# Two transformer blocks on one core: norms with tokens on partitions in the delta rule and in forgetting attention, another rule for placing the first stage's small steps, and the pooled products one chunk sooner

## What is computed

```python
fq = rmsnorm(heads(fq, FOX_HEADS), fox_qnorm[l])
fk = rmsnorm(heads(fk, FOX_HEADS), fox_knorm[l])
...
ya = fox_attention(fq, fk, heads(fv, FOX_HEADS), logf)
...
def step(state, xs):
    q_n, u_n, w_n, g_n, attn_n, kt_n, gl_n = xs
    v_new = u_n - jnp.einsum("bhck,bhkv->bhcv", w_n, state)
    o = (jnp.einsum("bhck,bhkv->bhcv", q_n * jnp.exp(g_n)[..., None], state)
         + jnp.einsum("bhce,bhev->bhcv", attn_n, v_new))
    state = state * jnp.exp(gl_n)[..., None, None] + jnp.einsum("bhck,bhcv->bhkv", kt_n, v_new)
    return state, o
...
yb = (rmsnorm(o, gdn_onorm[l]) * jax.nn.silu(heads(gz, GDN_HEADS).astype(f32)))
...
mixed = (g[..., 0, :] * (ya @ w_oa[l]) + g[..., 1, :] * (yb @ w_ob[l])
         + g[..., 2, :] * (yc @ w_oc[l]))
```

## Time and profile before

| | |
|---|---|
| median of 3 runs | 1172.26 us (1172.22 to 1172.81) |
| the profiled execution, whole | 1173.59 us |
| its span, first to last instruction | 1171.9 us |
| mean granted TensorE clock | 0.995 |
| PE busy | 1149.0 us, 98% |
| DVE busy | 811.6 us, 69% |
| ACT busy | 620.9 us, 53% |
| POOL busy | 81.9 us, 7% |

### The profile page before, as it was taken

One profiled execution on the slowest core, in us unless ns is written; L12 is line 12 of the kernel. 1 busy time (PEld: TensorE's weight loads), 2 busy tenths in 40 slices (PEclk: granted clock), 3 DMA queues, 4 the chain that ended last, 5 costly groups with the idle time before them and its releaser, 6 DMA issues.

```text
span 1171.9 us, 16827 instructions
## 1 busy us (share of the span) xinstructions
PE 1149.0 (98%) x6777; PEld 1003.8 (86%) x6777; DVE 811.6 (69%) x880; ACT 620.9 (53%) x799; POOL 81.9 (7%) x114
## 2 busy tenths in 40 slices
PE   8999999999999999999999999999999999999997
PEld 7978998889987899999888888888777888888886
DVE  6897668756877668787458777547776747777743
ACT  7666446436477566565345444436456547444432
POOL 7101100200000000000000000002600000000000
PEclk9999999999999999999999999999999998999999
DMA  8654233334664445654656655655633534666560
GB/s 259 193 156 149 96 108 109 108 109 155 221 198 146 144 162 164 196 184 177 220 175 188 207 180 181 214 180 188 197 108 127 180 108 127 192 202 182 178 214 36
DMA packets 144420, 193.95 MB, mean 166 GB/s; under 512 B 6168, under 2 KB 121240, under 8 KB 144344
## 3 DMA queue, kind: packets, MB, share of 16 engines
q1 hardware_dynamic: 143144, 188.43, 49.9%
q0 software_dynamic: 1200, 4.46, 1.1%
HBM read 191.82 MB, written 1.05 MB: 165 GB/s over the span
## 4 chain that ended last, share of the span: by engine, by line
PE 83%; DVE 9%; ACT 4%; issue 3%; DMA 0%; DVEq 0%; ACTq 0%
PE banks L1344 23%; PE banks L1378 19%; PE banks L1326 13%; PE banks L1347 11%; PE banks L1363 3%; DVE wlo L1956 3%; PE banks L1354 2%; PE banks L1615 1%; ACT whi L1675 1%; PE banks L1502 1%; PE banks L1489 1%; PE banks L1392 1%; PE banks L1573 1%; PE banks L1333 1%; PE banks L1570 0%
## 5 line engine op out<-in xcount | busy, mean ns | idle before, releaser
L1956 DVE TENSOR_TENSOR wlo<-raw,whi 128x2048 fp32r<-128x2048 f32 (+1 forms) x178 | 406.6, 2292 | 123.9 <-ACT whi L1675 123.8
L1675 ACT ACTIVATE whi<-raw 128x2048 fp32r<-128x2048 f32 (+1 forms) x179 | 340.1, 1903 | 252.8 <-PE banks L1347 147.3
L1344 PE MATMUL banks<-xhl,whi 128*128 128x512 f32 x1232 | 396.5, 403 | 1.6 <-DVE y5l L2289 1.3
L1347 PEld LDWEIGHTS banks<-xhl,wlo 128*128 128x128 f32 x1232 | 231.4, 188 | 54.6
L1347 PE MATMUL banks<-xhl,wlo 128*128 128x256 f32 x1232 | 242.6, 278 | 0.0
L1344 PEld LDWEIGHTS banks<-xhl,whi 128*128 128x128 f32 x1232 | 189.0, 189 | 8.7 <-issue 5.8
L1326 PE MATMUL banks<-xhl,whi 128*128 128x256 f32 x912 | 165.5, 284 | 1.1 <-DVE xhl L1984 0.6
L1326 PEld LDWEIGHTS banks<-xhl,whi 128*128 128x128 f32 x912 | 142.0, 192 | 2.0 <-DVE xhl L1984 1.0
L1326 PE MATMUL banks<-xhl,wlo 128*128 128x256 f32 x456 | 129.0, 283 | 0.0
L1378 PE MATMUL banks<-whi,hh 128*128 128x512 f32 x264 | 102.9, 390 | 0.0
L1378 PE MATMUL banks<-wlo,hh 128*128 128x512 f32 x264 | 102.7, 389 | 0.0
(11 more groups left out here) (369 smaller groups left out, 1537.1 us busy)
## 6 DMA issues: line engine op xcount, KB each, us to landing
raw<-in_w_in SPq DMA_DIRECT2D x40, 1024.0 KB, 5.3
raw<-in_w_up SPq DMA_DIRECT2D x22, 1024.0 KB, 5.4
raw<-in_ffn_w_gate SPq DMA_DIRECT2D x22, 1024.0 KB, 5.3
raw<-in_ffn_w_up SPq DMA_DIRECT2D x22, 1024.0 KB, 5.3
raw<-in_ffn_w_down SPq DMA_DIRECT2D x22, 1024.0 KB, 5.1
raw<-in_w_down SPq DMA_DIRECT2D x11, 1024.0 KB, 5.1
raw<-in_w_out SPq DMA_DIRECT2D x8, 1024.0 KB, 5.2
raw<-in_xa_wkv SPq DMA_DIRECT2D x8, 1024.0 KB, 5.5
```

The source lines that it names most:

```text
L1344: pe.matmul(bank(b[m]), wh[:, k, m * P:(m + 1) * P], both[:, k, :, :].rearrange("p a t -> p (a t)"), start=(k == 0), stop=(k == KD - 1), s ...
L1347: ins = pe.matmul(bank(b[m])[:, 0:T], wl[:, k, m * P:(m + 1) * P], Xh[:, k, :], start=False, stop=(k == KD - 1), skip_group_check=True)
L1675: act.activation(columns(whi, c, part), columns(raw, c, part), ACT.Copy).then_inc(act_done, 1)
L1956: dve.tensor_tensor(columns(wlo, c, part), columns(raw, c, part), columns(whi, c, part), ALU.subtract).then_inc(dve_done, 1)
```

## The change

- **Forgetting attention's norms.** The fq and fk projections become V chunks, tokens on partitions, and so are copied out by ACT and not added by DVE. `token_norm` squares them on ACT, sums each head on DVE (`tn_red`), takes the root of 8 numbers a token on ACT, multiplies on DVE (`tn_mul`), and PE turns the eight 128x128 blocks (`tn_t`), which ACT writes out with the gain (`tn_e`). The four `hn` norms with their matmuls by ones go.
- **The delta rule's end.** gz becomes a V chunk pair. `g_bc`, `g_egc` and `g_qg`, which spread exp(g) over the partitions and scaled q, go: exp(g) comes as a fourth column of `gcols` and the last decay by one small matmul in `rows6`; `r_ws` also makes q times the state, with tokens on partitions, `r_q` scales it on ACT, and `r_oc` adds it on DVE. The norm of the result is `n_sq`, `n_red`, `n_r`, `n_mul`, with 128 tokens on partitions; for the first tile it rides on links of `gdn(1)`. At the end `n_t` turns both tiles, and `n_h` and `n_l` write the two parts directly; `hn("go0", "go1")` and the `yh`, `yl` of this branch go.
- **The placing of links** in the first stage: `EARLY["rows"]` and `EARLY_LONG` become 0, the rough costs are edited, and `drain()` before the O chunks goes: the long chain has to be finished only for the third branch.
- **`mem_load`** is issued after the third branch's first O chunk and not after the first branch.
- **The mixer.** `pl_mm` moves from the middle of the third qk chunk to the middle of the second V chunk, into banks 2 and 3, and the hook between `pl_h` and `pl_l` goes. In both MoBA lanes `pn` of the first head joins the link of its `sc`.
- `g_vb` and `z_lk` do the same work with fewer DVE instructions.

The diff, cut to its core (the table of rough costs and declarations of tiles are left out):

```diff
-EARLY, EARLY_LONG = {"rows": 0.5, "mem": 0.5, "moba": 0.5, "xa": 0.5}, 0.6
+EARLY, EARLY_LONG = {"rows": 0.0, "mem": 0.5, "moba": 0.5, "xa": 0.5}, 0.0
...
     for what, c0 in (("fq", FQ), ("fk", FK)):
-        for i in range(2):
-            wide(win, c0 + 256 * i, "x", "add", to=what, i=i)
+        vals(win, c0, "x", "vcopy", to=what)
...
-    for i in range(2):
-        wide(win, GZ + 256 * i, "x", "add", to="gz", i=i)
+    vals(win, GZ, "x", "vcopy", to="gz")
...
-                            i=i, banks=(2 * i, 2 * i + 1), evac="gated"))
+                            i=i, banks=(2 - 2 * i, 3 - 2 * i), evac="gated"))
...
-    ready = {f"y{br}": [("yl", br)] for br in range(3)}
+    ready = {f"y{br}": [("yl", br)] for br in (0, 2)}
+    ready["y1"] = [("n_l", 0), ("n_l", 1)]
...
+        if name == "tn_t":
+            return pl.ended.get(("hn_mul", "gk1"), 1e9)
...
+        if name == "n_mul":
+            return pl.ended.get(("gzs",), 1e9)
...
+    def token_norm(m):
+
+        return [[("act", "tn_sq", m), ("dve", "tn_red", m), ("act", "tn_r", m)], [("dve", "tn_mul", m)],
+                [("pe", "tn_t", m), ("act", "tn_e", m)]]
+
...
-        c += [[("pe", "g_uw", t), ("dve", "g_u", t), ("act", "g_w", t)],
-              [("pe", "g_bc", t), ("act", "g_egc", t), ("dve", "g_qg", t)]]
-        c += [[("pe", "r_ws", t), ("dve", "r_vn", t)],
-              [("pe", "r_o", t), ("act", "r_oc", t), ("dve", "r_s", t)]]
+        c += [[("pe", "g_uw", t), ("dve", "g_u", t), ("act", "g_w", t)]]
+        c += [[("pe", "r_ws", t), ("dve", "r_vn", t), ("act", "r_q", t)],
+              [("pe", "r_o", t), ("dve", "r_oc", t), ("dve", "r_s", t)]]
         return c
+
+    def delta_out(t):
+
+        return [("act", "n_sq", t)], [("dve", "n_red", t)], [("act", "n_r", t)], [("dve", "n_mul", t)]
 
...
+        if kind == "moba":
+            links = [links[0] + links[1]]
...
     a += hn("gq0", "gk0", "gq1", "gk1")
-    for t in range(2):
-        a += gdn(t)
-    a += hn("go0", "go1")
+    a += gdn(0)
+    second = gdn(1)
+    for link_, norm_ in zip(second, delta_out(0)):
+        link_ += norm_
+    a += second
+    n_sq, n_red, n_r, n_mul = delta_out(1)
+    a += [n_sq + n_red + n_r, n_mul, [("pe", "n_t", 0), ("pe", "n_t", 1), ("act", "n_h", 0), ("dve", "n_l", 0), ("act", "n_h", 1), ("dve", "n_l", 1)]]
...
-    b += hn("fq0", "fq1", "fk0", "fk1")
+    b += token_norm("fq") + token_norm("fk")
...
-    drain()
+    for t in range(2):
+        pl.take(("n_t", t), (4 + t,), ("n_l", t))
...
-        if nth == 0:
-            pl.add("act", "yh", BRANCHES[2])
-            pl.add("dve", "yl", BRANCHES[2])
...
-        if nth == 0:
-            pl.add("pool", "mem_load")
         if nth == 1:
             pl.add("dve", "premix")
+        if nth == 2:
+            pl.add("pool", "mem_load")
         c += 2
...
     mm(c)
-    mm(c + 1)
-    pl.take(("pl_mm",), (0, 1), ("pl_l",))
-    mm(c + 2, mid=[("pe", "pl_mm"), lambda: low_part(True), ("act", "pl_h"), hook, ("dve", "pl_l")])
+    pl.take(("pl_mm",), (2, 3), ("pl_l",))
+    mm(c + 1, mid=[("pe", "pl_mm"), lambda: low_part(True), ("act", "pl_h"), ("dve", "pl_l")])
+    mm(c + 2)
     mm(c + 3)
...
-            return bank(g % 2)[:, (g // 2) * T:(g // 2 + 1) * T]
+            return bank(2 + g % 2)[:, (g // 2) * T:(g // 2 + 1) * T]
...
-                pool.wait_ge(pe_done, at("mm", chunk_of("gated", 1) - 4, 1))
+                pool.wait_ge(pe_done, at("mm", chunk_of("gated", 1) - 1, 1))
...
-                    for j, row in enumerate((BETA, BEGC, ETAIL)):
-                        o = (t * 3 + j) * 4
-                        ins = pe.transpose(bank(4)[:, o:o + 4], row[:, t * P:(t + 1) * P], ident[0:4, 0:4])
-                ins.then_inc(pe_done, 1)
+                    for j, row in enumerate((BETA, BEGC, ETAIL, EGC)):
+                        o = (t * 4 + j) * 4
+                        pe.transpose(bank(4)[:, o:o + 4], row[:, t * P:(t + 1) * P], ident[0:4, 0:4])
+                pe.matmul(bank(4)[:, 32:40], ones[0:4, :], last_decay, start=True, stop=True).then_inc(pe_done, 1)
...
+            def tn_t(m):
+
+                pe.wait_ge(dve_done, at("tn_mul", m))
+                if m == "fq":
+                    pe.wait_ge(dve_done, at("hn_mul", "gk1"))
+                else:
+                    pe.wait_ge(act_done, at("tn_e", "fq"))
+                src = TO[m]
+                for t in range(NT):
+                    for h in range(NH):
+                        ins = pe.transpose(bank(6 + t)[:, h * P:(h + 1) * P], src[:, t, h * P:(h + 1) * P], ident[:, :])
+                ins.then_inc(pe_done, 1)
...
             def r_ws(t):
                 pe.wait_ge(act_done, at("g_w", t))
-                pe.wait_ge(dve_done, at("g_qg", t))
+                pe.wait_ge(dve_done, at("g_u", t))
+                s = slice(t * P, (t + 1) * P)
                 for h in range(NH):
-                    ins = pe.matmul(bank(4)[:, h * P:(h + 1) * P], gU[:, h, :], gS[:, h, :], start=True, stop=True)
+                    pe.matmul(bank(4)[:, h * P:(h + 1) * P], gU[:, h, :], gS[:, h, :], start=True, stop=True)
+                for h in range(NH):
+                    ins = pe.matmul(bank(5)[:, h * P:(h + 1) * P], gq_[:, h, s], gS[:, h, :], start=True, stop=True)
                 ins.then_inc(pe_done, 1)
 
             def r_o(t):
-                s = slice(t * P, (t + 1) * P)
                 pe.wait_ge(dve_done, at("r_vn", t))
+                pe.wait_ge(act_done, at("r_q", t))
                 for h in range(NH):
-                    o = bank(5)[:, h * P:(h + 1) * P]
-                    pe.matmul(o, gS[:, h, :], gq_[:, h, s], start=True, stop=False)
-                    pe.matmul(o, gMs0[:, h, :], gAT[:, h, :], start=False, stop=True)
+                    pe.matmul(bank(5)[:, h * P:(h + 1) * P], gAT[:, h, :], gMs0[:, h, :], start=True, stop=True)
                 for h in range(NH):
                     ins = pe.matmul(bank(4)[:, h * P:(h + 1) * P], gKt[:, h, :], gMs0[:, h, :], start=True, stop=True)
+                ins.then_inc(pe_done, 1)
+
+            def n_t(t):
+
+                pe.wait_ge(dve_done, at("n_mul", t))
+                pe.wait_ge(dve_done, at("r_s", 1))
+                for h in range(NH):
+                    ins = pe.transpose(bank(4 + t)[:, h * P:(h + 1) * P], go_[:, t, h * P:(h + 1) * P], ident[:, :])
                 ins.then_inc(pe_done, 1)
...
-                    pe.wait_ge(dve_done, at("hn_mul", "fk1"))
-                    pe.wait_ge(dve_done, at("hn_mul", "gk1"))
+                    pe.wait_ge(act_done, at("tn_e", "fk"))
...
+            def tn_sq(m):
+
+                act.wait_ge(act_done, at("copy", chunk_of(m, None)))
+                if m == "fk":
+                    act.wait_ge(dve_done, at("tn_red", "fq"))
+                act.activation(S1[:, :], TO[m][:, 0, :], ACT.Square)
+                act.activation(PT1[:, :], TO[m][:, 1, :], ACT.Square).then_inc(act_done, 1)
+
+            def tn_r(m):
+                act.wait_ge(dve_done, at("tn_red", m))
+                link(act.activation(token_root, token_root, ACT.Ln, bias=eps, scale=1.0 / HD))
+                act.activation(token_root, token_root, ACT.Exp, scale=-0.5).then_inc(act_done, 1)
+
+            def tn_e(m):
+
+                act.wait_ge(pe_done, at("tn_t", m))
+                act.wait_ge(dve_done, at("params_c"))
+                gain = gsc if m == "fq" else pcolumn("fox_knorm")
+                for t in range(NT):
+                    ins = act.activation((fq_ if m == "fq" else fk_)[:, :, t * P:(t + 1) * P], per_head(bank(6 + t)), ACT.Copy, scale=gain)
+                ins.then_inc(act_done, 1)
...
+                if t and l == 1:
+                    act.wait_ge(dve_done, at("n_red", 0))
...
+            def r_q(t):
+                act.wait_ge(pe_done, at("r_ws", t))
+                for h in range(NH):
+                    hs = slice(h * P, (h + 1) * P)
+                    ins = act.activation(go_[:, t, hs], bank(5)[:, hs], ACT.Copy, scale=gcols[:, t, 3, h:h + 1])
+                ins.then_inc(act_done, 1)
+
+            def n_sq(t):
+
+                act.wait_ge(dve_done, at("r_oc", t))
+                act.activation(gU[:, :, :], per_head(go_[:, t, :]), ACT.Square).then_inc(act_done, 1)
+
+            def n_r(t):
+                act.wait_ge(dve_done, at("n_red", t))
+                link(act.activation(onr[t], onr[t], ACT.Ln, bias=eps, scale=1.0 / HD))
+                act.activation(onr[t], onr[t], ACT.Exp, scale=-0.5).then_inc(act_done, 1)
+
+            def n_h(t):
+                act.wait_ge(pe_done, at("n_t", t))
+                act.wait_ge(pe_done, at("z_o", NH - 1))
+                act.activation(ybh[1][:, :, t * P:(t + 1) * P], per_head(bank(4 + t)), ACT.Copy,
+                               scale=pcolumn("gdn_onorm")).then_inc(act_done, 1)
...
+                for t in range(NT):
```

(50 more changed lines are left out.)

78 lines of the change are left out of this document (29 added, 49 removed).

## The result

The changed kernel takes 1182.89 us (median of 4, 1180.70 to 1183.35) against 1172.53 us: a ratio of 1.0082, 95% interval 1.0068 to 1.0095. That is 10.4 us slower, where I had forecast 10 us faster. The profiled execution took 1182.82 us, its span 1181.1 us.

The account below looks back on a forecast made before the run. PE was taken as the bound, busy 1149.0 of 1171.9 us. Terms -5.5 (PE work), -1.2 (placing) and -3.3 (mixer) sum to -10.0 us; from the median 1172.26 that gives 1162.3 us, range 1159.2 to 1168.0.

Parts of the forecast that it names:

- PE work, -5.5: Mostly first-stage PE instructions that go and come, such as hn_sum, g_bc and transposes: -5.5 us, hardly depending on the order.
- The -1.2 us that the placing was to win from waits: First stage: links placed only when their input is there win part of 1.8 us of PE waits: -1.2 us.
- So I let every `l_x` of both tiles slip once, and five others: Delta rule's long chain: 17 missed quarters at 1.4 us, 24 us later, less savings, ending near 282 us.
- five others: Five links of the long chain besides the l_x, each slipping once at 1.4 us.
- That is why the missing `drain()` costs nothing: After the gates: the chain ends 18 us before the third branch needs it, so dropping drain() costs nothing.
- The rival "slower": Chain not done when the third branch is due, links forced with PE idle; with eight, 1182 us. Chance 0.03.
- The tables among the sigmoids: Rival: n_r of the second tile after the first gsig, two more ACT table loads, 2 x 1.28 us: 1164.9 us. Chance 0.14.
- The mixer, -3.3: Second block's mixer: potential of 4.6 us from two waits and slow clock, 1.3 given back: -3.3 us.
- The 1.34 us may thus shrink or stay: Mixer: PE's 1.34 us wait for pl_l before the last qk chunk was to shrink or stay.
- The 1.7 us of slow clock: Mixer: 1.7 us lost to PE's clock of 0.66 after the wait before pt; was to go with that wait.
- `mem_load`: Issued three O chunks later, at 307 us, with 16 us to land before ACT reads the memory: cost 0.

Follow-up runs that it names:

- a_old_mixer: The changed kernel with the second block's mixer as before the change: 1179.77 us, ratio 1.0058.
- d_three_costs: The changed kernel with old placing and old mixer, and only the costs cv_add, cv_silu and hn_mul at their old values: 1167.12 us, ratio 0.9951.
- c_old_costs: The changed kernel with old placing, old mixer and all fifteen edited costs of steps that both kernels have at their old values: 1171.12 us, ratio 0.9988.
- d_old_costs_placing_03: c_old_costs with EARLY for the rows at 0.3 in place of 0.5: 1165.81 us, ratio 0.9941.
- a_old_both: The changed kernel with both the old placing and the old mixer, new costs kept: 1173.59 us, ratio 1.0006.
- d_drain: The changed kernel with drain() put back after the gates and nothing else: 1187.51 us, ratio 1.0128.
- a_old_placing: The changed kernel with EARLY for the rows back at 0.5 and EARLY_LONG at 0.6, drain() still missing: 1176.33 us, ratio 1.0031.
- c_best_merge: c_old_costs with one part of the new mixer, pn in the link of its sc: 1172.43 us, ratio 0.9998.
- e_after_old_costs: The changed kernel with the fifteen old costs and nothing else, new placing and new mixer kept: 1181.01 us, ratio 1.0060.
- e_03_mixer: d_old_costs_placing_03 with pn in its sc's link and no hook between pl_h and pl_l, pl_mm at its old place: 1165.31 us, ratio 0.9929.
- e_03_nohook: d_old_costs_placing_03 with only the hook between pl_h and pl_l taken out, no merge of pn: 1166.24 us, ratio 0.9939.
- d_three_costs_mixer: d_three_costs with pn in its sc's link and no hook between pl_h and pl_l, pl_mm at its old place: 1165.34 us, ratio 0.9939.

## Why the prediction was wrong

Step by step from the changed kernel: the mixer costs 3.1 us (a_old_mixer), placing and three costs together 1179.8 - 1167.1 = 12.7 us (from there to d_three_costs), and what is left is 1167.1 - 1172.85 = -5.7 us, the last against the kernel before on the same chip. I had -3.3, -1.2 and -5.5. (The top of my range should have read 1168.3 by its own sum; the measured time is far above either.)

- **PE work, -5.5: right in kind, a little small.** d_three_costs is 5.3 us ahead at norm_mem's turn and 5.7 in the median, but its first stage has 3.4 us of waits against 2.0 before. From 55 us to that turn PE is busy for 263.6 us against 270.4, both at a clock of 1.00, so its work is 6.8 us less, and the nearness of 5.7 to my 5.5 is in part luck. Nor is it true that this part hardly depends on the order: the same instructions take 264.6 us in c_old_costs and 262.2 in d_old_costs_placing_03. The -1.2 us that the placing was to win from waits didn't come. The token norms don't make the chain late.
- **"So I let every `l_x` of both tiles slip once, and five others": this step failed.** I took 24 us of slip, less 5 and 4, and an end near 282 us. `g_uw` of the second tile alone came 39.3 us late. The levels did what I had said: the second tile's six `l_x` take 36.6 us (243.3 to 279.9) against 29.4 (211.2 to 240.6), 1.4 us a step, and both tiles' together 14.3 us more, where I had 12 x 1.4 = 16.8. The "five others", 7 us in my sum, are what was mis-sized: the first tile's `g_turn` is 15.2 us late already, and from its `g_uw` to the second tile's first `l_x` it takes 62.7 us (180.6 to 243.3) against 50.4 (160.8 to 211.2), 12.3 us more. With the three costs undone `g_turn` stands at 101.4 us instead of 117.4 (d_three_costs and a_old_both), so the first piece lies in the steps ahead of it, the convolution (`cv_add`, `cv_silu`) and the norms of q and k (`hn_mul`). Of the 9 us that I took off the chain (5 for `g_bc`, 4 for the result's norm) little came at its end: from the second tile's `g_uw` to the end of the norm it takes 20.7 us (282.1 to 302.8) against 23.8 (242.9 to 266.6). Why a link loses more than the quarter that it misses stays my reading, that it has several DVE or ACT steps; no run has it alone. I treated the placing as one number that each link meets once. It acts through the planner's clocks together with the cost table, and that table, part of the change, has no term in my sum at all. Undone singly in the changed kernel, the costs are worth 1.9 us, which the intervals don't tell from nothing, and the placing 6.6; undone together (three costs) 12.7.
- **"That is why the missing `drain()` costs nothing": right for the wrong reason.** The chain was not done 18 us before the 300.5 us at which I had the branch start, but at 305.6, 5 us after, and PE had no weight product left from 291.2 us on; the missing drain then saved 4.6 us (d_drain).
- **The rival "slower", 0.03, is what happened,** at 1182.9 us to my 1182. Its price was partly luck: I had eight forced links at 2.5 us, and there were three, with 11.0 us of idle PE, a clock near half from 295 to 310 us, and two table loads and `premix` inside. Its condition, a chain 34 us later, was the right one, and I gave it too little since my slip had no row under it.
- **The tables among the sigmoids** came too, as part of that wait: 2 x 1.28 us before `n_mul`. The load at 306.57 us is the one that the kernel before has at 302.88.
- **The mixer, -3.3: wrong sign, 2.7 to 3.1 us lost.** The wait before `pt` shrank from 1.51 to 0.75 us; I had it gone. The failed step is the place of `pl_l`: "The 1.34 us may thus shrink or stay". It grew to 2.84 us. In a_old_placing, whose wait is the same (2.82), `pl_mm` is done at 847.2, but ACT has the next chunk's `hi` and two lane steps (a copy of PT and an `ex`) ahead of `pl_h`, which starts only at 849.26, and `pl_l` ends at 852.60 (in the changed kernel the same: 852.7, 854.80 and 858.13):

```profile
845.78 1.90 ACT L1708 ACTIVATE whi<-raw 128x2048 fp32r<-128x2048 f32 x1
...
849.26 1.57 ACT L2010 ACTIVATE y5h<-banks,pcol 128x256 fp32r<-128x256 f32 x4
```

  The 1.7 us of slow clock did not go either. They moved behind the new wait: 0.81 over 856 to 861 us and 0.84 over the next 5 us in the changed kernel, 0.66 in c_best_merge. I had taken back half of two waits and nothing for the clock. That part is not bound to the wait, though. In e_after_old_costs, with the same mixer, a wait of 3.09 us for `pl_l` is followed by a clock of 1.00, and the mixer takes 60.3 us from its first `sc` to the last heads against 62.5 in the changed kernel and 60.5 before. Likewise 1.50 us before `pt` are followed by 0.66 in a_old_both and 1.52 us by 1.00 in a_old_mixer. So some 1.7 us of my potential and of the measured loss hang on something that I didn't control.
- **`mem_load`: no loss shown.** It is issued at 313.95 and ACT reads the memory at 329.76, without a wait on the load; no run moved it alone.

**Open.** The last norm, which the planner calls the seam, begins with a wait of PE (before: 0.61 us, up to 975.06 us). From there to the end eleven of the seventeen kernels take 195.97 to 197.00 us and six, the changed one among them, 197.78 to 198.07. All six have an edited mixer, but e_03_mixer (196.66), e_03_nohook (196.65) and d_drain (196.71) have one too, and no edit is of a step behind the mixer. What differs is when PE runs at the lower clock behind the same waits. In d_three_costs:

```profile
973.00:975.00 2.00, 2.00 (x11) 2.00 (x11) 1.13 (x5) 1.87 (x8) 0.00 (x0) 0.50 0.72 225
975.00:977.00 2.00, 2.00 (x17) 2.00 (x17) 0.73 (x2) 1.54 (x1) 0.00 (x0) 0.83 0.09 37
```

and in d_three_costs_mixer, 1.1 us earlier in time:

```profile
972.00:974.00 2.00, 2.00 (x11) 2.00 (x11) 1.22 (x4) 1.87 (x7) 0.00 (x0) 0.50 0.63 221
974.00:976.00 2.00, 2.00 (x12) 2.00 (x11) 0.62 (x2) 1.44 (x1) 0.00 (x0) 0.50 0.10 41
976.00:978.00 2.00, 2.00 (x13) 2.00 (x12) 0.14 (x1) 0.48 (x2) 0.00 (x0) 0.58 0.00 0
```

What decides it stays open. It means that 1.3 us between two of these kernels can come from a place that the edit didn't touch: each half of the mixer has 1.0 us of its 1.3 there, and of the 3.1 us between the changed kernel and a_old_mixer 1.3 us are there (197.98 against 196.64).

## What to carry to other kernels

When a planner places work by estimated times, its cost table and its tolerance are as much a part of a diff as the instructions: a long chain turned a few tenths of a microsecond of caution into 39 us, so find the latest time at which the chain may end, and read in the trace how late it is after its first third. Let it run early rather than late, but not with costs below the real ones, since then each link waits on PE. And a wait removed from a chain of several engines is a gain only if what PE comes to next is ready sooner too: ask for the queue of each engine ahead of that operand.

## What the runs showed of the hardware

- Behind the sigmoids, Ln and the Exp after it each loaded a table of their own (298.19 and 299.80 us, 1.28 us each). The Trainium skill, ScalarE: Activation LUTs, section "Table sets: the hidden batching unit", has one set with both, so that Ln and then Exp should need one load. The trace differs where nothing preloads that set; the measurement decides. Where the kernel asks for that set by name (L1700, the load at 53.04 us), six times Ln with Exp behind it runs before the next load at 160.20 us.
- With three waits that left PE idle for 11.0 us within 12.7 us its granted clock was 0.50 to 0.59 from 295 to 310 us, though it was busy for 4.14 of the last 5 us.
- The same wait can be followed by either clock: waits of 1.54 and 2.00 us in the mixer of d_old_costs_placing_03 and of 3.09 us in e_after_old_costs by 1.00, waits of 1.50 us in a_old_both and 2.84 us in the changed kernel by 0.66 (842 to 847 us) and 0.81 (856 to 861 us). At 0.66 over 5 us the difference is 1.7 us, between stretches with nearly the same work. No run here shows what decides it.
